# The compressed branch's 64 matmuls read their moving operand three times: 135 columns instead of 45

## The reference, cut to what matters

```python
CMP_LEN, CMP_STRIDE = 32, 16
n_cmp = (S - CMP_LEN) // CMP_STRIDE + 1          # 15
starts = jnp.arange(n_cmp) * CMP_STRIDE
tok = starts[:, None] + jnp.arange(CMP_LEN)[None, :]

def compress(a, pos, w1, w2):
    blk = a[:, tok] + pos[:, None, :]
    blk = blk.transpose(0, 1, 3, 2, 4).reshape(B, n_cmp, G, CMP_LEN * Dh)
    return jax.nn.gelu(blk @ w1) @ w2

Kc = rms_norm_2(compress(kc, cmp_pos[0], cmp_w1[0], cmp_w2[0]), k_g[0])
Vc = compress(vc, cmp_pos[1], cmp_w1[1], cmp_w2[1])
```

## Time and profile before

| | |
|---|---|
| median of 3 executions | 2694.69 us (2689.23, 2694.69, 2694.78) |
| profiled execution, its own time | 2686.35 us |
| its span, first to last instruction | 2684.6 us |
| mean granted TensorE clock | 0.97 of full speed |
| TensorE matmul busy | 2534.9 us (94%) |
| VectorE, ScalarE, GpSimd busy | 1781.3, 857.7, 362.9 us |

### The profile page before, as it was taken

The page is one execution under the profiler, slowest core; times in us unless marked ns, Lnnn a source line. Parts: engine busy times, 40 slices in busy tenths (PEclk is TensorE's granted clock), DMA queues, the critical chain, the costliest instruction groups (busy, mean ns, idle before and its releaser), DMA issues.

```text
span 2684.6 us, 45593 instructions
## 1 busy us (share of the span) xinstructions
PE 2534.9 (94%) x17164; PEld 2372.1 (88%) x17164; DVE 1781.3 (66%) x3554; ACT 857.7 (32%) x2170; POOL 362.9 (14%) x384
## 2 busy tenths in 40 slices
PE   5968999978999999999999999999999999999998
PEld 4857888867888888899999999999888999999998
DVE  6885664695465553599888874412746998878744
ACT  2532210244211022212665540122432126655300
POOL 0230110022010001002111121100220021111211
PEclk8989999999999999999999999978999999999999
DMA  8325887520687862379999999924013899999998
GB/s 325 132 79 212 306 305 286 185 79 22 235 302 273 310 244 92 118 272 399 356 401 388 407 404 415 414 79 149 25 63 126 292 382 373 406 383 409 404 415 339
DMA packets 171355, 725.21 MB, mean 270 GB/s; under 512 B 19024, under 2 KB 19536, under 8 KB 146384
## 3 DMA queue, kind: packets, MB, share of 16 engines
q1 hardware_dynamic: 143568, 522.10, 52.6%
q0 software_dynamic: 27648, 201.34, 18.5%
HBM read 722.32 MB, written 1.05 MB: 269 GB/s over the span
## 4 chain that ended last, share of the span: by engine, by line
PE 76%; issue 8%; DVE 8%; DMA 5%; ACT 2%; POOL 0%; SPq 0%; DVEq 0%; ACTq 0%; POOLq 0%
PE banks L724 32%; PE banks L970 21%; PE lev L1012 17%; DMA ring<-in_peer_v 4%; PE lev L724 2%; PE lev L953 1%; PE banks L953 1%; DVE arena L1810 1%; PE lev L1037 1%; DMA extra<-in_ada 1%; DVE arena L1804 1%; DVE nmax L1696 1%; DVE arena L1823 1%; DVE arena L1821 1%; DVE arena L1635 1%
## 5 line engine op out<-in xcount | busy, mean ns | idle before, releaser
L724 PE MATMUL banks<-hT,ring 128*128 128x256 f32 x2832 | 631.4, 386 | 37.1 <-ACT hT L1196 36.7
L724 PEld LDWEIGHTS banks<-hT,ring 128*128 128x128 f32 x2832 | 549.2, 194 | 118.0 <-issue 40.8
L1012 PE MATMUL lev<-arena,ring 128*128 x4096 | 580.3, 302 | 4.5 <-DMA ring<-in_peer_v 4.2
L970 PE MATMUL banks<-hT,ring 128*128 128x160 f32 x4096 | 580.0, 302 | 0.0
L1012 PEld LDWEIGHTS lev<-arena,ring 128*128 128x128 f32 x4096 | 559.4, 191 | 7.8 <-issue 7.6
L970 PEld LDWEIGHTS banks<-hT,ring 128*128 128x128 f32 x4096 | 562.1, 191 | 0.9 <-issue 0.3
L1606 POOL DMA_INDIRECT arena<-in_peer_rows,keysb x192 | 204.7, 1066 | 1156.6 <-DVE consts L1952 630.7
L724 PE MATMUL banks<-arena,ring 128*128 128x256 f32 (+1 forms) x1344 | 287.7, 379 | 2.5 <-DMA ring<-in_stream_first 2.5
L724 PEld LDWEIGHTS banks<-arena,ring 128*128 128x128 f32 x1344 | 254.9, 200 | 33.9 <-issue 2.9
L1996 DVE SCALAR_TENSOR_TENSOR extra<-consts,chT 128x192 bf16<-128x192 f32 x640 | 223.3, 407 | 7.9 <-ACT arena L1287 7.7
L724 PE MATMUL lev<-arena 128*128 128x128 f32 (+1 forms) x976 | 155.6, 310 | 39.9 <-DVE arena L1810 31.3
(11 more groups left out here) (274 smaller groups left out, 2418.0 us busy)
## 6 DMA issues: line engine op xcount, KB each, us to landing
ring<-in_peer_u SPq DMA_DIRECT2D x256, 512.0 KB, 7.7
ring<-in_peer_v SPq DMA_DIRECT2D x256, 512.0 KB, 9.2
ring<-in_stream_first SPq DMA_DIRECT2D x192, 512.0 KB, 3.7
arena<-in_ada SPq DMA_DIRECT2D x104, 512.0 KB, 5.2
extra<-in_ada SPq DMA_DIRECT2D x88, 512.0 KB, 4.8
ring<-in_stream_nsa SPq DMA_DIRECT2D x45, 512.0 KB, 3.3
ring<-in_stream_fox SPq DMA_DIRECT2D x41, 512.0 KB, 3.5
arena<-in_peer_rows,keysb POOLq DMA_INDIRECT x192, 8.6
```

The source lines that it names most:

```text
L724: ins = nc.tensor.matmul(o, lhsT, rhs, start=start, stop=stop, **kw)
L970: ins = nc.tensor.matmul(banks[k // 2 % 4][:, (k % 2) * ND:(k % 2 + 1) * ND], ring[:, u % RING, c], hT[:, c, NS:T], start=c == 0, stop=c = ...
L1012: ins = nc.tensor.matmul(lev[c // 4][:, (c % 4) * T + NS:(c % 4 + 1) * T], ring[:, u % RING, c], a[:, bass.ds(g, 1), k], start=False, stop ...
```

## The change

The moving operand gets one more axis of length 3 with a step of zero in front of its axes. Each matmul so reads the same 45 elements three times over and writes 135 columns instead of 45 into the same PSUM bank. Weights, number of matmuls, order, waits and signals stay the same; ScalarE reads the same 31 columns as before, and nothing reads columns 45 to 134. All outputs are unchanged.

```diff
                         last = l == CMP_LEN - 1
-                        mm(bm[:, 0:3 * N_CMP], w[:, l % 8],
-                           kvc[:, kv, :, l:l + CMP_STRIDE * (N_CMP - 1) + 1:CMP_STRIDE], l == 0, last,
+                        x = kvc[:, kv, :, l:l + CMP_STRIDE * (N_CMP - 1) + 1:CMP_STRIDE]
+                        mm(bm[:, 0:9 * N_CMP], w[:, l % 8], x.unsqueeze(1).broadcast_to([P, 3, 3, N_CMP]), l == 0, last,
                            filled("cmp", kv)[0] if last else None)
```

## The result

The changed kernel takes 2698.1 us at the median of 12 executions; the kernel before, executed in turn with it, 2692.2. The ratio is 1.0023 with a 95% interval of 1.0012 to 1.0033: slower by 6.2 us, 3.2 to 8.9. One execution of each kernel took far longer than its others (9262.4 and 3014.4 us), and the ratio leaves these two out. The forecast was +3.8 us, a time of 2698.5, and a range of 2684 to 2703. The gain that the clock could give is there, and the price of the wide columns, somewhat over the forecast's upper bound, takes more than all of it.

The account below looks back on a forecast made before the run. TensorE's stream was taken to bound the kernel. Stage +5.5 us and the records behind it -1.7 give +3.8, so the median of 2694.7 becomes 2698.5 us; range 2684 to 2703.

Parts of the forecast that it names:

- The clock: In the stage of 128 changed records: granted clock 1.00 throughout, where it was 0.50 for 17.2 us.
- the 1.7 us behind it: The 32 records of 256 columns behind the stage: 6.90 us at full clock instead of 8.61.
- Rival 3: Clock falls to 0.50 in the stage and some 3 us behind: 29.1 us, nothing given back, 2701.4 us; chance 0.08.
- The streaming time: In the changed stage: reads 64 bytes apart cost 0.80 ns instead of 0.42, no longer hidden under the weight load.
- 218 ns a record: Each 135-column record: 270 reads at 0.80 ns plus 2.3 ns; 128 of them make a stage of 27.9 us.
- The upper bound of 227 ns: Highest price of a 135-column record: two full clocks a read, 0.833 x 270 + 2.3; stage 29.1 us.
- Rival 2: The second record's start, 60 ns after the first, shows the streaming time: 176 ns a record, 2693.1 us; chance 0.15.
- Rival 1: Wide stream is cheap, the 34 ns excess a fixed hidden cost: 115 ns a record, -9.4 us, 2685.3 us; chance 0.17.
- Rival 4: Some other addition, as a repeated axis costing more than its elements or a wait for weights: over +5.4 us; chance 0.06.
- The limit of the narrow streams: On TensorE, up to about 128 contiguous columns a record costs the same, put down to its weight load of 128 columns.
- +5.5: The stage of 128 changed records: 27.9 us instead of 22.4.

Follow-up runs that it names:

- the contiguous control: The kernel before with 45 contiguous columns read in place of 45 at a step of 64 bytes; stage 22.17 us, no ratio given.
- the last kernel: Kernel before with the threefold innermost repeat, bias expansion widened from 48 to 96 columns and compressed scores from 15 to 60; ratio 0.9894, 2662.0 us.

## Why the prediction was right, and which term was off

**What bounds the kernel.** Right: TensorE's stream does. What a stage gained or lost came out in the whole, by stages and by ratio: +5.4 and +6.2 us in the changed kernel, -9.4 and -7.0 with the innermost repeat of 3, -9.8 and -10.2 with that of 2, -4.2 and -5.4 with the outermost of 2, -9.8 and -11.3 at 60 columns. Each figure by stages lies within the interval of its ratio, and no new pause showed up to attention in the changed kernel.

**The clock.** Right, in the stage and behind it: 1.00 in both, and the 1.7 us behind it came back as reckoned (6.92 us against 6.90 forecast). Rival 3 is out. What was a choice between neighbouring rows is now shown by runs: in the two kernels with 45 columns, contiguous or not, the clock fell to 0.50 within the stage; in those with 60, 90, 135 and 180 slow columns it was 1.00 from the first record to the last. Why it falls with 45 stays open.

**The streaming time.** The mechanism was right, and its size was off, in the term "218 ns a record". Measured are 230.5: each slow read costs 0.838 ns instead of the 0.80 read from the first record's length, and a record 4.6 ns besides instead of 2.3. On 270 reads that makes 12 ns, on 128 records 1.6 us. The upper bound of 227 ns, two clocks and the contiguous stream's 2.3 ns, was too low as well, since it took the extra per record from a stream without slow reads. Rival 2 (176 ns, from the start of the second record) is out. In the outermost repeats of 2, 3 and 4 the second record starts 0.14, 0.22 and 0.29 us after the first, as it did 0.06 us after it with 45 columns, and the flow then settles at 155, 230 and 306 ns. From 90 to 360 reads that is 0.23 us more for 270 reads more, 0.85 ns a read. So the 60 ns held the full price of the slow reads, less some 10 to 20 ns by which the second start comes early at every width; rival 2 took the 60 ns for the price itself and tripled it. The rows from the second record on, of the kernels with 90, 135 and 180 columns:

```profile
1814.51 0.49 PE L724 MATMUL banks<-arena,ring 128*128 128x90 f32 x2
```

```profile
1818.11 0.41 PE L724 MATMUL banks<-arena,ring 128*128 128x135 f32 x1
```

```profile
1814.41 0.48 PE L724 MATMUL banks<-arena,ring 128*128 128x180 f32 x1
```

**Rivals 1 and 4.** Rival 1, a fixed cost that the flow hides, is out by the kernels with 90, 135 and 180 columns. But one reason that the prediction gave against it was wrong: that 289 ns in steady flow against 276 show the slow reads. Contiguous columns of the same count show 287. The reason that held was the first record, 238 ns, of which the contiguous control shows 203. That this excess grows with the reads was a choice in the prediction and is shown now. Rival 4 asked for over +5.4 us, and the +6.2 us by ratio is in its region, but neither of its mechanisms is there: no new idle time stands on TensorE, and a kernel without a repeated axis (one run at 16 bytes) costs 240 ns. What isn't separated is whether some of the 4.6 ns that a record costs beside its reads comes from the repeated axis.

**The limit of the narrow streams.** That up to about 128 contiguous columns a record costs the same is borne out by the last kernel, at clock 1.00: 19.17 us / 172 = 111.5 ns at 96 contiguous columns, 7.09 us / 64 = 110.8 ns at 60, with 115.2 at 135 just above. In 60 slow columns and 90 paired ones it is 111.3 and 111.4. That this is the weight load was argued in the prediction and not tried. Also not tried: what slow reads cost at half clock (the prediction's 227 ns); no wide kernel's stage ran at half clock.

**The sum.** Forecast +5.5 - 1.7 = +3.8; the stages show +7.1 - 1.7 = +5.4. That the forecast time of 2698.5 us is only 0.4 us from the measured 2698.1 is luck in part: it starts from 2694.7 us, and the kernel before took 2692.2 when the two were executed in turn, while the change itself cost some 2 us more than forecast. The chances put 0.58 on no measurable change and 0.25 on slower; it came out slower by 0.23%, just past the bound of 0.2%, with an interval that reaches to both sides of it. The idea of the change was sound, and its width and order weren't: of 230 ns a record half goes when the same repeat stands innermost.

## What to carry to other kernels

Look at the granted clock even where TensorE is always busy: here the back-to-back float32 streams of 15, 45 and 48 columns ran for a part at 0.50, and columns that nobody reads brought all three to 1.00. They cost nothing as long as their streaming time stays under what sets the record's cost (112 ns here). Widen by repeating the innermost element or contiguous columns; a repeat outside a strided pattern paid two clocks for each read again (0.838 ns). Price a strided moving operand by a contiguous control: against it the first record's length and the start of the second showed the slow reads, and the lengths in steady flow didn't.

## What the runs showed of the hardware that was not expected

The price of a strided float32 read isn't monotonic in the step: 240 ns a record at 16 bytes, 230 at 64, 120 at 8, 115 contiguous (135 columns each). The one at 64 bytes also differs in its axes and its repeat, so it isn't shown that the step alone makes these 10 ns.

Weight loads are longer beside the slow reads where these set the record's cost: the loads of the changed kernel take 206 ns at the median, those of the kernel with the innermost repeat 189. The weight loads of the changed kernel in 4 us of the stage, and then those of the other, both at full clock:

```profile
L724 PEld LDWEIGHTS banks<-arena,ring x18: 206/206/206, 1820.9 to 1824.8; 128*128 128x128 f32 x18
```

```profile
L724 PEld LDWEIGHTS banks<-arena,ring x37: 189/189/190, 1820.9 to 1825.0; 128*128 128x128 f32 x37
```

It isn't the slow reads as such. At 60 slow columns, where a record costs 111.3 ns, the loads take 192 ns:

```profile
L724 PEld LDWEIGHTS banks<-arena,ring x37: 192/192/192, 1814.9 to 1818.9; 128*128 128x128 f32 x37
```

Whether the longer load is a cause or only goes with the record's 4.6 ns beyond its reads stays open.
